# Attention loop: where TensorE takes scores, turns, spreading and values

## The reference

```python
q_a = rope(rmsnorm_2(q_a), pos); k_a = rope(rmsnorm_2(k_a), pos)
o_a = banded_attention(q_a, k_a, v_a, A_WINDOW - 1, sinks=sinks_a)   # softmax over 0 <= i-j <= 127, plus the sink
o_a = o_a * silu(g_a)
q_b = rope(rmsnorm_2(q_b), pos); k_b = rope(rmsnorm_2(k_b), pos)
o_b = dilated_attention(q_b, k_b, v_b)     # patterns (128, 1), (512, 4), (2048, 16), merged by their denominators
o_b = o_b * silu(g_b)
x = x + concatenate([o_a, o_b]) @ w_out
```

## Time and profile before

| | |
|---|---|
| median of 3 runs | 2329.57 us |
| profiled execution, its own time | 2330.13 us |
| its span | 2328.3 us |
| first to last matmul of the attention loop | 2051.15 to 2224.6 us, 7% of the span |
| TensorE busy, whole span | 2098.6 us (90%) |
| VectorE, ScalarE, GpSimd busy | 68%, 53%, 28% |
| mean granted TensorE clock | 0.959 of full speed |

### The profile page before, as it was taken

How to read it: one execution, slowest core, us unless ns; L and a number is a source line. 1 busy time by engine, 2 the same in 40 slices (tenths; PEclk the granted TensorE clock), 3 DMA queues, 4 the chain that set the end, 5 groups by cost and what they waited for, 6 DMA issues and landing times. The chain is left out here.

```text
span 2328.3 us, 51472 instructions
## 1 busy us (share of the span) xinstructions
PE 2098.6 (90%) x21654; PEld 1673.0 (72%) x21654; DVE 1575.8 (68%) x2324; ACT 1245.5 (53%) x2324; POOL 655.5 (28%) x465
## 2 busy tenths in 40 slices
PE   5999999599999988891899999999958999999989
PEld 3788887577888853781688888888747778866667
DVE  3566654788888746426599999999756846656531
ACT  5422221466677654442687888888545444357530
POOL 0000020565666610114013313313025465400011
PEclk8999999799999999995899999999979999999999
DMA  8222251333323239426699999999645374340032
GB/s 287 59 68 75 65 130 39 75 71 72 71 67 67 46 126 337 146 106 235 215 353 384 386 392 388 383 397 389 235 145 191 103 229 115 92 131 2 3 109 82
DMA packets 164786, 399.63 MB, mean 172 GB/s; under 512 B 13630, under 2 KB 58060, under 8 KB 164556
## 3 DMA queue, kind: packets, MB, share of 16 engines
q1 hardware_dynamic: 149932, 347.56, 43.0%
q0 software_dynamic: 12224, 44.57, 7.0%
q10 hardware_dynamic: 2400, 4.21, 0.5%
HBM read 348.06 MB, written 46.66 MB: 170 GB/s over the span
## 5 line engine op out<-in xcount | busy, mean ns | idle before, releaser
L1930 DVE TENSOR_TENSOR exp_w_lo<-exp_w,exp_w_hi 128x2048 fp32r<-128x2048 f32 x186 | 414.3, 2288 | 24.0 <-ACT exp_w_hi L1887 23.8
L1887 ACT ACTIVATE exp_w_hi<-exp_w 128x1024 fp32r<-128x1024 f32 x384 | 377.7, 1052 | 68.6 <-PE banks L1849 48.4
L2142 POOL TENSOR_TENSOR w_lo<-mixT,w_hi 128x512 fp32r<-128x512 f32 (+1 forms) x108 | 144.1, 1356 | 169.9 <-ACT w_hi L2218 165.9
L1849 PE MATMUL banks<-exp_w_hi,xsT_lo 128*128 128x512 f32 x512 | 161.0, 396 | 6.3 <-DVE xsT_lo L1934 6.3
L1849 PE MATMUL banks<-exp_w_lo,xsT_hi 128*128 128x512 f32 x512 | 159.4, 393 | 0.0
L1849 PE MATMUL banks<-exp_w_hi,xsT_hi 128*128 128x512 f32 x512 | 159.3, 393 | 0.0
L1817 POOL DMA_INDIRECT moe_rows<-exp_out,idxT x16 | 25.2, 1573 | 439.2 <-DVE exp_out L1989 439.2
L2200 PE MATMUL banks<-w_hi,h_lo 128*128 128x512 f32 (+1 forms) x320 | 122.1, 382 | 7.8 <-POOL w_lo L2142 5.3
L1802 POOL DMA_INDIRECT xs<-xn_rows,idxT x16 | 116.0, 7247 | 14.2 <-DVE idxT L1961 5.6
L2200 PE MATMUL banks<-w_hi,h_hi 128*128 128x512 f32 (+1 forms) x320 | 119.1, 372 | 0.0
L2200 PE MATMUL banks<-w_lo,h_hi 128*128 128x512 f32 (+1 forms) x320 | 119.0, 372 | 0.0
(11 more groups left out here) (384 smaller groups left out, 5584.2 us busy)
## 6 DMA issues: line engine op xcount, KB each, us to landing
exp_w<-in_exp_w_gate_dram SPq DMA_DIRECT2D x64, 1024.0 KB, 10.1
exp_w<-in_exp_w_up_dram SPq DMA_DIRECT2D x64, 1024.0 KB, 10.4
exp_w<-in_exp_w_down_dram SPq DMA_DIRECT2D x64, 1024.0 KB, 7.8
mixT<-in_w_in_dram SPq DMA_DIRECT2D x96, 256.0 KB, 2.9
ada_w_second<-in_ada_w_dram SPq DMA_DIRECT2D x16, 1024.0 KB, 9.5
chunk<-rkv_scratch SPq DMA_DIRECT2D x80, 192.0 KB, 4.0
w_in_ring<-in_w_in_dram SPq DMA_DIRECT2D x26, 512.0 KB, 4.0
rkv_scratch<-work POOLq DMA_DIRECT2D x16, 640.0 KB, 6.6
```

The lines of the kernel that those rows point to most:

```text
L1849: mm = pe.matmul(g.ps[bank + q][:, :], lhs[:, kk, :], wide[:, k, q * 512:(q + 1) * 512], start=(kk == 0 and p == 0), stop=(kk == KT - 1 an ...
L1887: last = act.activation(wh[:, n % RH, k, :], w[:, n % RING, k, :], ACT.Copy)
L1930: dve.tensor_tensor(wl[:, n % RH, :, :], w[:, n % RING, :, :], wh[:, n % RH, :, :], ALU.subtract).then_inc(lo_ok, 1)
L2142: pool.tensor_tensor(wl[:, q % SR, 0:width(q)], w[:, q % WR, 0:width(q)], wh[:, q % SR, 0:width(q)], ALU.subtract).then_inc(w_lo, 1)
```

## The change

Only the order of TensorE's steps in one round changes. No instruction is added or taken away, no wait is edited, and the other engines keep their order. Value(p - 2) comes directly behind score(p). Both turns of pair p - 1 follow. Widen comes last and is now that of pair p - 1, one pair earlier than before.

```diff
@@ -2547,13 +2547,12 @@
             for p in range(NPAIR + 2):
                 if p < NPAIR:
                     score(p)
+                if p >= 2:
+                    value(p - 2)
                 if 1 <= p < NPAIR + 1:
                     turn(2 * p - 2)
-                if p >= 2:
-                    widen(p - 2)
-                    value(p - 2)
-                if 1 <= p < NPAIR + 1:
                     turn(2 * p - 1)
+                    widen(p - 1)
```

## The result

| | before | changed |
|---|---|---|
| median, 20 runs each | 2331.02 us | 2337.89 us |
| lowest to highest | 2324.91 to 2337.07 | 2330.07 to 2342.68 |
| ratio | | 1.0025 (95%: 1.0016 to 1.0034) |
| profiled execution, own time / span | 2330.13 / 2328.3 us | 2333.55 / 2331.7 us |

The changed kernel is slower by 0.25%, 3.7 to 7.9 us by the interval; the forecast was 2336.5 us. The loss is clear of zero, and its interval straddles the line of 0.3%. Two more comparisons agree: 1.0027 (1.0013 to 1.0041) for the same kernel again, 1.0033 (1.0018 to 1.0048) for a near relative (`e2`).

The account below looks back on a forecast made before the run. TensorE was taken to bound the attention loop, setting the 2.17 us round with every wait already satisfied. New waits of 1.0 + 3.2 + 1.5 + 0.1 + 0.8 = 6.6 us gave 2336.5 us, range 2330.5 to 2341.

Parts of the forecast that it names:

- the line of 0.3%: Whole kernel: a measurement can tell about 0.3%, 7.0 us; the forecast loss was said to lie almost on it.
- TensorE's own work unchanged: Full round of half A: groups without waits sum to 2.16 us against 2.17, with four shape changes in either order.
- far rounds: Rounds 40 to 62, with far keys: nothing waits, 0.1 us in all, at worst 1.2.
- Value waits for the second copy: Full rounds of half A: value, now earlier, waits for ScalarE's second copy; round 2.24 us, +0.07.
- Widen waits for the reciprocal in narrow rounds: Half A, t = 1 and 2: widen can't start before 1.76 us, making rounds 2.13, +0.18 and +0.17.
- rounds 8 to 31: Three full sets of eight rounds in half A, each +1.08 from the new waits: +3.2 us.
- rounds 32 to 39: First rounds of half B, up to its first far keys: the new waits add 1.5 us.
- tail: After the last score: no score hides a copy, so value(63) comes at 9.01 us instead of 8.17, +0.8.
- The start: Rounds 0 to 7: an extra widen in round 1 (+0.37) and the new waits, +1.0 us; waits rarer at half clock.
- it might fall elsewhere: Rival: half-clock stretches at both ends of the stage fall differently, 4 us less in all, 2332.5 us; chance 0.10.
- The rival of a clock falling inside the stage: New waits drop TensorE's clock inside the attention stage; up to 1.6 us a stretch, four make 2342.9; chance 0.05.
- The sum: Attention stage: 1.0 + 3.2 + 1.5 + 0.1 + 0.8 = 6.6 us added.

Follow-up runs that it names:

- e2: Changed order, with VectorE's reciprocal of pair p - 1 taken ahead of both softs of p instead of behind them; 1.0033 (1.0018 to 1.0048) of the kernel before.
- three shape experiments: Widen alone moved to round's end (1.0076); changed order with widen kept before value (1.0007); old order with turns together, value last (0.9990); ratios to the kernel before.
- e1: Changed order, with the copy of each pair's second side moved from ScalarE to VectorE behind its reciprocal; 1.0016 (0.9999 to 1.0033) of the kernel before.
- e3: Order before, with both turns together, then widen(p - 2) and value(p - 2) last; 0.9990 (0.9976 to 1.0004) of the kernel before.
- e7: Old order in rounds 0 to 7, changed order from round 8 on; 1.0028 (1.0016 to 1.0040) of the kernel before.
- e4: Order before, with only widen moved, as that of pair p - 1, to the end of the round; 1.0076 (1.0051 to 1.0102) of the kernel before.
- e6: Order score, both turns, widen(p - 2), value(p - 2), with the second side's copy on VectorE; 2323.14 us against 2329.66 for the kernel before, 0.9979.

## Why the prediction was right

- **TensorE's own work unchanged**: right. Value 0.58 to 0.59, turns 0.59, widen 0.37 were each as forecast. In the far rounds, where nothing waits, the 23 rounds went from 80.85 to 81.20, 0.015 each. The three shape experiments bear out the price of about 0.10 for a change of shape and 0.05 for value behind one, in both directions. So does the step from 128 to 32 rows inside one value of the kernel before, 0.10. This agrees with the rule, from the Trainium skill's page "TensorEngine Tiling (Array Packing)", Key Properties, that a change of tiling mode drains TensorE: five, four and three changes gave 2.33, 2.18 (`e1`) and 2.03 (`e3`). These are rounds without a wait. The traces show the price; the drain itself they don't show.
- **Value waits for the second copy**: right, with 2.26 for 2.24, and shown by `e1`.
- **Widen waits for the reciprocal in narrow rounds**: right, 2.15 for 2.13, and shown by `e2`. It is not additive, though. Taken away alone it returns 0.2 us per eight rounds, not 0.35, for value's wait takes it back.
- **Sizes**: rounds 8 to 31 +3.6 (forecast 3.2), rounds 32 to 39 +1.35 (1.5), far rounds +0.35 (0.1), tail +0.8 (0.8). These make 6.1 where the prediction had 5.6.
- **The start** is the term that was mis-sized: +2.2, +4.5 and +1.7 in three profiles for a forecast of +1.0. The working took the stretch at half clock as given, said waits would be rarer in it, and weighed only that it might fall elsewhere. It didn't ask whether the new order feeds it. With the stretch beginning equally late (first profile) 3.4 us more of it cost up to 1.7 us. The rival of a clock falling inside the stage didn't come true; from round 4 on no profile but those with 13.7 us has half clock before value(63).
- **The sum**: 8.3 us in the stage of the first profile, 6.6 forecast, +6.9 between the medians, 5.8 (3.7 to 7.9) by the ratio. The stage's +8 to +11 in three profiles and the smaller ratio don't quite meet. The first score came at 2048.5 us on average in the three profiles of the changed kernel and at 2052.3 in the four of before; with a scatter of 4 to 5 us among either, and 2046.1 us in `e7`, whose first rounds are the old ones, I can't tell whether that is more than chance. It is also open how often the stretch begins early in the timed runs of either kernel. That the forecast time lies so near the measured one is in part luck: the start was priced 0.7 to 3.5 us too low, the other stages 0.5 too low, and the ratio shows less than any profile's stage.

## What to carry to other kernels

- An engine that is busy all the time with all its waits satisfied has slack that no busy share shows. Before moving a step earlier, write down when its input is ready and how far behind that it starts: here 0.49 us of slack paid for nothing, and a move of 0.64 turned it into a wait in most of the first 40 rounds.
- On TensorE, count the changes of array shape in a round and keep groups of one shape together, but only in an order in which the consumer of a copy still comes late. With turns together and widen in front of value at the end, plus one copy moved to an engine with room, the kernel became 0.2% faster than before.

## What the hardware showed that I had not expected

The order of work in the first microseconds of a stage can change how long TensorE's clock stays at half. Where the stretch began 3.7 to 3.9 us behind the first score, it lasted 3.4 us in all five profiles with the old start and 6.8 us in the two with the changed one (changed, `e2`), at about 2 us of time. Where it began 1.9 to 2.1 us behind, it lasted 6.8 or 13.7 us in six profiles, none of them with the old start, at up to 4.5 us in the changed kernel.

A short wait for weights in the output stage can bring the half clock back: in `e4` and `e6`, one profile each, TensorE waited 2.78 and 2.01 us for the last output weights, and 1.3 us behind the end of that wait (`e4`) or right at it (`e6`) the clock fell to half for 3.4 us. From value(63) to the end they took 109.3 and 108.5 us, where before took 105.2 to 105.5. Waits of up to 1.5 us at the same place, in the other profiles, were not followed by such a stretch.
